# The Gated DeltaNet convolution inputs in 512-column products with sums in PSUM, and a new order of casts and low parts

## The reference

```python
proj = jnp.einsum('bsd,de->bse', hn, w_in[l])
(fq, fk, fv, ff, gq, gk, gv, ga, gb, gz, gate_fox, gate_gdn) = split_in(proj)
log_f = jax.nn.log_sigmoid(ff.astype(jnp.float32) + fox_f_bias[l].astype(jnp.float32))
qkv = jax.nn.silu(causal_dwconv(jnp.concatenate([gq, gk, gv], axis=-1), gdn_conv_w[l]))
cq, ck, cv = jnp.split(qkv, [GDN_K_WIDTH, 2 * GDN_K_WIDTH], axis=-1)
q = l2norm(cq.reshape(B, S, GDN_HEADS, GDN_HEAD_K))
k = l2norm(ck.reshape(B, S, GDN_HEADS, GDN_HEAD_K))
v = cv.reshape(B, S, GDN_HEADS, GDN_HEAD_V)
g = -jnp.exp(gdn_a_log[l].astype(jnp.float32)) * jax.nn.softplus(
    ga.astype(jnp.float32) + gdn_dt_bias[l].astype(jnp.float32))
beta = jax.nn.sigmoid(gb.astype(jnp.float32))
```

## Time and profile before

| | us |
|---|---|
| median of three runs (1611.69 to 1614.2) | 1613.13 |
| the profiled execution | 1614.05 |
| its span, first to last instruction | 1612.3 |
| TensorE busy in it | 1564.9 |
| VectorE busy | 629.7 |
| ScalarE busy | 499.2 |
| GpSimd busy | 291.2 |

### The profile page before, as it was taken

One profiled execution on the slowest core, in us unless ns is written; L12 is line 12 of the kernel. 1 busy time (PEld: TensorE's weight loads), 2 busy tenths in 40 slices (PEclk: granted clock), 3 DMA queues, 4 the chain that ended last, 5 costly groups with the idle time before them and its releaser, 6 DMA issues. The chain is left out here.

```text
span 1612.3 us, 21430 instructions
## 1 busy us (share of the span) xinstructions
PE 1564.9 (97%) x8406; PEld 882.2 (55%) x8406; DVE 629.7 (39%) x1177; ACT 499.2 (31%) x795; POOL 291.2 (18%) x179
## 2 busy tenths in 40 slices
PE   9999999999999999999999999999999999999998
PEld 8843333333333333323233233588899888888886
DVE  7742212121212212112121121396476456658752
ACT  6431111111111111111101111366556553467753
POOL 2600000000000000000000000274333323435552
PEclk9999999999999999999999999999999999999999
DMA  9699999999999999999999999644234234556552
GB/s 349 233 380 354 427 427 427 427 427 426 428 426 428 427 428 426 427 428 428 428 428 428 428 428 427 248 157 157 78 115 144 84 105 162 205 167 212 180 187 104
DMA packets 94889, 507.67 MB, mean 315 GB/s; under 512 B 10059, under 2 KB 35448, under 8 KB 70104
## 3 DMA queue, kind: packets, MB, share of 16 engines
q1 hardware_dynamic: 94568, 505.97, 77.8%
q10 hardware_dynamic: 240, 0.55, 0.1%
HBM read 505.46 MB, written 1.05 MB: 314 GB/s over the span
## 5 line engine op out<-in xcount | busy, mean ns | idle before, releaser
L190 POOL TENSOR_TENSOR low<-ring,high 128x1024 fp32r<-128x1024 f32 x81 | 201.7, 2491 | 1261.9 <-ACT high L187 1261.8
L1741 PE MATMUL ps<-ring,x 128*64 128x512 f32 x1536 | 341.9, 595 | 20.9 <-DMA ring<-in_w_up 20.9
L1741 PEld LDWEIGHTS ps<-ring,x 128*64 128x64 f32 x1536 | 106.0, 137 | 252.7 <-issue 207.0
L187 ACT CAST high<-ring 128x1024 fp32r<-128x1024 f32 x162 | 168.0, 1052 | 110.0 <-PE ps L1993 28.4
L1782 PE MATMUL ps<-ring,x 128*64 128x512 f32 x752 | 172.0, 600 | 1.2 <-issue 0.8
L190 DVE TENSOR_TENSOR low<-ring,high 128x1024 fp32r<-128x1024 f32 x81 | 107.4, 1326 | 95.0 <-ACT high L187 94.3
L1584 DVE TENSOR_SCALAR hT<-ps 128x512 f32<-128x512 f32 x32 | 22.1, 692 | 291.7 <-PE ps L1741 291.7
L1741 PE MATMUL ps<-extra,x 128*64 128x512 f32 x512 | 114.6, 595 | 5.8 <-DMA extra<-in_w_up 5.8
L1958 PE MATMUL ps<-hTb,high 128*128 128x512 f32 x464 | 116.4, 393 | 0.5 <-PEq L2917 0.5
L1782 PEld LDWEIGHTS ps<-ring,x 128*64 128x64 f32 x752 | 52.5, 138 | 100.7 <-issue 100.0
L1651 ACT COPY gpickT<-ps 128x256 f32<-128x256 f32 x32 | 11.9, 373 | 282.1 <-PE ps L1761 282.1
(11 more groups left out here) (518 smaller groups left out, 2302.8 us busy)
## 6 DMA issues: line engine op xcount, KB each, us to landing
ring<-in_w_down SPq DMA_DIRECT2D x52, 2048.0 KB, 32.7
ring<-in_w_gate SPq DMA_DIRECT2D x48, 2048.0 KB, 31.2
ring<-in_w_up SPq DMA_DIRECT2D x47, 2048.0 KB, 31.1
ring<-in_w_in SPq DMA_DIRECT2D x22, 2048.0 KB, 7.9
extra<-in_w_gate SPq DMA_DIRECT2D x16, 2048.0 KB, 31.4
extra<-in_w_up SPq DMA_DIRECT2D x16, 2048.0 KB, 29.7
extra<-in_w_down SPq DMA_DIRECT2D x14, 2048.0 KB, 34.5
ring<-in_w_up SPq DMA_DIRECT2D x24, 1024.0 KB, 7.2
```

What stands on the lines that cost most here:

```text
L187: eng.copy(hi, self.raw(u)).then_inc(self.sem("high_split"), 1)
L190: eng.tensor_tensor(lo, self.raw(u), hi.bitcast(F32), ALU.subtract).then_inc(self.sem(who + "_split"), 1)
L1741: last = pe.matmul(bank[h * CAP:(h + 1) * CAP, :], xg[:, c, kh, :], w[:, c, h * 512:(h + 1) * 512], start=False, stop=kh == 1 and c == 3)
```

## The change

The pieces gq, gk and gv of both groups go through `columns_wide`; each unit has a bank of its own, and the bank plan is stretched accordingly. fq, fk, fv and gz stay as they were. The convolution works chunk by chunk (256 columns, one unit): ScalarE copies the bank's second half to the new buffer `whole_conv`, VectorE adds it onto the first half in PSUM, ScalarE writes the last tap with a scaled copy, VectorE adds the three other taps. Two chunks overlap on VectorE. The semaphores `chunk_taken` and `chunk_sum` count the hand-overs, and the w_up stage goes on counting on them. On ScalarE, in group 0, the copy of the gate columns stands between q chunks 1 and 2; k chunks 0 and 1 stand in the gate rows, between the first exponentials and the logarithms; the casts `ahead(7)` and `ahead(9)` stand ahead of the logarithms and after the gate exponentials. On VectorE k chunks 0 and 1 stand ahead of the wait for the logarithms, a low part `ahead(9)` after `beg`, and the rows' low parts move from ahead of gv to between its chunks 1 and 2.

```diff
@@ -1846,7 +1846,9 @@
     for hg in range(2):
-        for w in ("gq", "gk", "gv", "fq", "fk"):
+        for w in ("gq", "gk", "gv"):
+            piece("columns", [(w, hg, q) for q in range(4)])
+        for w in ("fq", "fk"):
             piece("columns", (None, (w, hg, 0), None, (w, hg, 1)))
...
@@ -1864,6 +1866,7 @@
 UNITS_GROUP, UNITS_E, UNITS_OUT = 28, 56, 88
+CONV_CHUNKS = 24
 
...
@@ -2057,6 +2060,7 @@
     gz = sb("gz", [P, NT, 512])
+    whole = sb("whole_conv", [P, 2, S])
     XT = sb("XT", [P, NT, HG, P])
...
@@ -2111,11 +2115,11 @@
 
-    banks.plan(*[("nm", j) for j in range(4)], "rt", ("rw", 0), ("rw", 1))
+    banks.plan(*[("nm", j) for j in range(4)])
     for hg in range(2):
-        banks.plan(("gq", hg, 0), ("gq", hg, 1), *([("oT", 0, 0), ("oT", 0, 1)] if hg else []),
-                   ("gk", hg, 0), ("gk", hg, 1),
-                   ("gv", hg, 0), ("gv", hg, 1), *([] if hg else ["cols"]),
+        banks.plan(*[("gq", hg, q) for q in range(4)], *([("oT", 0, 0), ("oT", 0, 1)] if hg else ["rt"]),
+                   ("gk", hg, 0), *([] if hg else [("rw", 0), ("rw", 1)]), *[("gk", hg, q) for q in range(1, 4)],
+                   *[("gv", hg, q) for q in range(4)], *([] if hg else ["cols"]),
                    ("fq", hg, 0), ("fq", hg, 1), *[("ss", hg, j) for j in range(4)], *[("rb", hg, h) for h in range(HG)],
...
@@ -2183,7 +2187,9 @@
                     chain(act.activation(temp[:, b, :], temp[:, b, :], ACT.Exp, scale=-1.0))
-                ahead(6)
+                for q in range(2):
+                    chunk(0, 1, q)
+                ahead(7)
                 for b in (TC, TD):
...
@@ -2194,6 +2200,7 @@
                 act.activation(temp[:, KD, 0:P], temp[:, KD, 0:P], ACT.Exp).then_inc(sem("eg_rows"), 1)
+                ahead(9)
                 banks.moved(act, ("rw", 1))
...
@@ -2207,26 +2214,45 @@
 
+            def chunk(hg, w, q):
+
+                n = 12 * hg + 4 * w + q
+                bank = banks.take(act, (("gq", "gk", "gv")[w], hg, q))
+                if n >= 2:
+                    act.wait_ge(sem("chunk_sum"), n - 1)
+                act.copy(whole[:, q % 2, :], bank[:, S:2 * S]).then_inc(sem("chunk_taken"), 1)
+                ahead(UNITS_GROUP * hg + 4 * w + q + 1)
+                act.wait_ge(sem("chunk_sum"), n + 1)
+                at = 17 + 24 * 3 + 8 * w + HG * hg + q
+                act.activation(gT[:, w, q, :], bank[:, 0:S], ACT.Copy, scale=prm2[:, at:at + 1])\
+                    .then_inc(sem("chunk_taken"), 1)
+
+            def silu(hg, w, j):
+
+                for q in (2 * j, 2 * j + 1):
+                    banks.moved(act, (("gq", "gk", "gv")[w], hg, q))
+                part = gT[:, w, 2 * j:2 * j + 2, :]
+                act.activation(part, part, ACT.Silu).then_inc(sem("g_silu"), 1)
+
             for hg in range(2):
 
                 u0 = UNITS_GROUP * hg
                 for w in range(3):
                     if hg and w == 1:
                         delta_high(0)
-                    for j in range(2):
-                        if hg == w == 0:
-                            if j == 0:
-                                ahead(4)
-                                gate_columns()
-                            else:
-                                ahead(5)
-                        else:
-                            ahead(u0 + 4 * w + 2 * j + 3)
-                        banks.moved(act, (("gq", "gk", "gv")[w], hg, j))
-                        part = gT[:, w, 2 * j:2 * j + 2, :]
-                        act.activation(part, part, ACT.Silu).then_inc(sem("g_silu"), 1)
+                    for q in range(4):
+                        if hg or w != 1 or q >= 2:
+                            chunk(hg, w, q)
+                        if hg == w == 0 and q == 1:
+                            gate_columns()
+                        if q == 1 and w and not (hg == 0 and w == 1):
+                            silu(hg, w - 1, 1)
+                    silu(hg, w, 0)
                     if hg == w == 0:
+                        ahead(5)
+                        silu(hg, 0, 1)
                         gate_rows()
+                silu(hg, 2, 1)
 
...
@@ -2434,8 +2460,7 @@
                 banks.release(last, ("rw", 0))
-                units.ahead(v, "low0", 6)
-                conv(1, "gk", 0, (0,))
+                conv(1, "gk", 0, range(2))
                 v.wait_ge(sem("rows_ln"), 2)
...
@@ -2454,27 +2479,35 @@
                 v.tensor_tensor(temp[:, BEG, P:S], temp[:, BEG, P:S], rowp[:, BETA, P:S], ALU.mult).then_inc(sem("beg"), 1)
-
-            def conv(w, name, hg, halves=(0, 1)):
-
-                for j in halves:
-                    units.ahead(v, "low0", UNITS_GROUP * hg + 4 * w + 2 * j + 2)
-                    bank = banks.take(v, (name, hg, j))
-                    for i in range(4):
-                        for a in range(2):
-                            ch = 8 * w + HG * hg + 2 * j + a
-                            c = gT[:, w, 2 * j + a, :]
-                            tap = prm2[:, 17 + 24 * (3 - i) + ch:18 + 24 * (3 - i) + ch]
-                            if i == 0:
-                                last = v.tensor_scalar(c, bank[:, a * S:(a + 1) * S], tap, None, ALU.mult)
-                            else:
-                                last = v.scalar_tensor_tensor(c[:, i:], bank[:, a * S:(a + 1) * S - i], tap, c[:, i:],
-                                                              ALU.mult, ALU.add)
-                            if i < 3:
-                                chain.mark(last)
-                        if i < 3:
-                            chain.wait()
-                    banks.release(last, (name, hg, j))
+                units.ahead(v, "low0", 9)
+
+            def conv(w, name, hg, chunks=range(4)):
+
+                def tap(q, i):
+
+                    bank = banks.take(v, (name, hg, q))
+                    c = gT[:, w, q, :]
+                    at = 17 + 24 * (3 - i) + 8 * w + HG * hg + q
+                    return v.scalar_tensor_tensor(c[:, i:], bank[:, 0:S - i], prm2[:, at:at + 1], c[:, i:], ALU.mult, ALU.add)
+
+                for q in [*chunks, None]:
+                    before = chunks[-1] if q is None else q - 1
+                    n = 12 * hg + 4 * w + before + 1
+                    if before >= chunks[0]:
+                        v.wait_ge(sem("chunk_taken"), 2 * n)
+                        chain.mark(tap(before, 1))
+                    if q is not None:
+                        bank = banks.take(v, (name, hg, q))
+                        v.wait_ge(sem("chunk_taken"), 2 * n + 1)
+                        v.tensor_tensor(bank[:, 0:S], bank[:, 0:S], whole[:, q % 2, :], ALU.add).then_inc(sem("chunk_sum"), 1)
+                    if before >= chunks[0]:
+                        chain.wait()
+                        chain.mark(tap(before, 2))
+                    if q is not None:
+                        units.ahead(v, "low0", UNITS_GROUP * hg + 4 * w + q + 1)
+                    if before >= chunks[0]:
+                        chain.wait()
+                        banks.release(tap(before, 3), (name, hg, before))
 
...
@@ -2492,14 +2525,17 @@
                     gate_rows()
-                conv(1, "gk", hg, (0, 1) if hg else (1,))
+                conv(1, "gk", hg, range(4) if hg else range(2, 4))
                 if hg == 0:
+                    conv(2, "gv", hg, range(2))
                     v.wait_ge(sem("row_high"), 2)
                     v.tensor_tensor(row_low[:, GC:BETA + 1, :], rowp[:, :, :], row_high[:, GC:BETA + 1, :].bitcast(F32),
                                     ALU.subtract).then_inc(sem("row_low"), 1)
                     v.tensor_tensor(row_low[:, NEGC, :], temp[:, TB, :], row_high[:, NEGC, :].bitcast(F32),
                                     ALU.subtract).then_inc(sem("row_low"), 1)
-                conv(2, "gv", hg)
+                    conv(2, "gv", hg, range(2, 4))
+                else:
+                    conv(2, "gv", hg)
 
...
@@ -2638,6 +2674,9 @@
 
+            def wide(u, name, hg, before=None, first=None):
+                columns_wide(pe, units, banks, u, [(name, hg, q) for q in range(4)], hTb, before, first)
+
             def both_t(u, name, hg, before=None):
...
@@ -2726,13 +2765,13 @@
                 u0 = UNITS_GROUP * hg
-                both_f(u0 + 0, "gq", hg, None, None if hg else splits_ready(k, pe, banks, "nm"))
+                wide(u0, "gq", hg, None, None if hg else splits_ready(k, pe, banks, "nm"))
                 if hg:
                     outputs_transposed(0)
                 else:
                     gate_columns()
-                both_f(u0 + 4, "gk", hg, None if hg else gate_rows)
-                both_f(u0 + 8, "gv", hg)
+                wide(u0 + 4, "gk", hg, None if hg else gate_rows)
+                wide(u0 + 8, "gv", hg)
                 if hg == 0:
...
@@ -3079,15 +3118,15 @@
                 if u >= 2:
```

(14 more changed lines are left out.)

## The result

The changed kernel takes 1616.55 us (median; 1613.95 to 1617.71) against 1613.44 for the kernel before (1611.16 to 1614.91) on the same chip: ratio 1.0019, 95% interval 1.0013 to 1.0026, so about 3.1 us more. The forecast was 1614.6, with 1607 to 1618 as its range, and "within 0.2%" as the likeliest case; the narrower range of the sum itself, 1612 to 1616, missed by 0.55. In a second comparison the same kernel had 1.0026 (1.0015 to 1.0036).

A forecast was written before the change was run, and what follows sets the result against it. The prediction took TensorE, busy 97% of the span, as the bound, with a 4.6 us hole at unit 12. Group 0 losing 2.6 and group 1 gaining 1.1 gave +1.5 on 1613.13: 1614.6 us, range 1607 to 1618.

The forecast's parts named there:

- Wide products: Groups 0 and 1: a wide unit takes 2.79 us instead of 2.88, saving 1.1 us in group 1.
- estimate of 0.24: Group 1's saving in us if a pair of products saves only 2.5 ns; the forecast would be 0.8 us longer.
- The rival that wide products are no faster: Wide products take as long as narrow ones, 1.1 us missing: 1615.7 us, inside the forecast; no chance of its own.
- Steps 1 to 5: Group 0 to unit 10: VectorE idle 4.1 us before k chunk 0, TensorE waiting 3 to 4.3 us at unit 10.
- Step 6: Group 0 at unit 13: TensorE waits about 1.5 us, then 0.5 for GpSimd's low part.
- a low clock after unit 10 is mostly swallowed here: Group 0 at unit 13: later waits there absorb most of the time a low clock after unit 10 costs.
- Step 7: End of group 0: silu, two casts and first square put the square sums at 1098.4 against 1095.82; loss taken as 2.6.
- What follows: After group 0's square sums: the shift passes on unchanged, group 1 has no waits and gains 1.1 us.
- 4.1 us of cover ... and the shift goes on one for one: After group 0's square sums: scaled q and k are ready 4.1 us before use, hiding ScalarE's 1 us extra lateness.
- The sum: Whole kernel: 2.6 lost in group 0 less 1.1 gained in group 1, +1.5 us, median 1614.6 us.
- TensorE-bound: Rival in group 0: ScalarE comes in time and no unit waits, 6.6 us less, 1606.5 us; chance 0.13.
- the slower rival: The clock falls to 0.50 at group 0's square sums, costing 1.6 us: 4.2 more in all, 1617.3 us; chance 0.21.

The follow-up runs named there:

- third version of the new order: Against the second version: q's squares behind v chunk 2, k's behind v chunk 3, VectorE copies fq's two banks instead of ScalarE; 1609.62 us against 1611.77 before, ratio 0.9985.
- second version: Against the first version of the new order: rows' low parts, row selector, v's first silu, squares and unit 17's cast moved; ratio to before 0.9992.
- first version of the new order: Changed kernel with casts and VectorE's low parts two units further ahead from k chunk 2, gate rows before silus, other reordering; ratio to before 1.0004.

## Why the prediction was right, and where it was not

*Wide products* (0.09 a unit): right. Twelve units of group 1 gave 0.99, expected 1.1. The estimate of 0.24 from the Trainium skill's page "TensorE: Matmul & The Clock Gate", section "Wait — 56ns, not 53.3ns?", differs from the measurement, and the measurement decides. The rival that wide products are no faster falls with it.

*Steps 1 to 5*: right within 0.6 us. VectorE's idle time before k chunk 0 was 4.64 for 4.1, unit 10's low part was done 38.4 us after unit 0 where the walk had 37.6 to 38.9, and TensorE waited 3.76 where 3 to 4.3 was forecast.

*Step 6* named two waits at unit 13 (1.5 and 0.5); in the profile above neither came. Its cast was done 47.55 us after unit 0 (47.3 walked), but the low clock behind unit 10 held TensorE until 48.28 (45.8 walked). That was chance: in the second profile of the same kernel unit 11's eight wide products took 2.39 us, not 3.41, TensorE came sooner, and both waits came, 0.23 on the cast and 0.32 on GpSimd's low part. The square sums were at 58.8 in both, so "a low clock after unit 10 is mostly swallowed here" was right; the waits were sized too long.

*Step 7*: right. Square sums +2.75 for +2.6, the wait there 1.70. The experiment with the squares ahead of the casts gives the two casts 1.5 of it, and the early low part of unit 10 shows that this end, not unit 10, sets the time in this kernel.

*What follows* is the step that failed, and with it the sum is 1 us short. "4.1 us of cover ... and the shift goes on one for one" looked at the scaled q and k, which are used first. The next use has less: the k transposes claim the third bank that VectorE frees. Before, that was 1.8 us ahead of them (its multiplication ended at 1113.88, the transposes began at 1115.66). After, ScalarE and VectorE are 1 us later than TensorE, as the text says itself, and both blocked decay products of 2.15 and 2.11 us now stand ahead of that bank, where only one did before:

```profile
1110.85 2.16 DVE L2533 TENSOR_TENSOR egb<-egb,gT 128x128 f32<-128x128 f32 x1
...
1113.47 0.41 DVE L2530 TENSOR_TENSOR xn<-xn,ps 128x256 f32<-128x256 f32 x1
...
1115.66 2.18 PE L2774 MATMUL ps<-ident,gT 128*128 128x128 f32 x16
```

These rows are of before (VectorE's first decay product, its third bank, TensorE's transposes); after has its rows above. So TensorE waits 0.71 there, and by the table the shift grows by 0.96 at the k transposes, of which 0.86 are left at unit 28. The experiment with the decay products behind takes out 0.66.

*The sum*: 2.6 - 1.1 = +1.5 was forecast; the distances give 2.75 + 0.86 - 0.99 = +2.6. Behind group 1 lies 0.24 more, from a wait of 0.23 at 1362.05 on a cast, behind a load that landed 0.2 later; before it is under 0.2, in the third version of the new order 0.52. Together 2.9, and the interval of the measured 3.1 (2.1 to 4.2) takes that in. Why the ratio lies above what the distances say for every kernel here, by 0.2 to 2.6 us, 1.1 in the mean, is not located: one profile of each can't show it. One thing to ask is the granted clock: the runs of before in the second comparison took 1613.3 to 1614.6 us at a mean granted clock of 0.995 and 1611.1 to 1612.3 at 0.998.

*The rivals*: TensorE-bound did not come by itself, but the third version, with the order changed and fq's copy on VectorE, gives 3.8 of the 6.6 us that it counted; its argument ("VectorE's work doesn't grow") was sound (busy 624.6 us after, 629.7 before), and "ScalarE's order" was the right reason against it. The clock at the square sums stayed at 1.00, so the slower rival's mechanism fell; that its time of 1617.3 was nearer than the forecast is luck. Its "no row shows a wait of that length" overlooked the kernel before at 141 to 143 us (last section).

## What to carry to other kernels

When a stage is handed from one engine to a chain of two, the chain's end can set the time, and a long wait of the main engine in the middle can be worth nothing: before removing it, ask what that engine meets next. When a shift is passed on, check the cover of every later claim, the banks too, not only that of the first use. In group 1, without gate rows, the wide products paid at once; in group 0 only when casts, table loads and silus of ScalarE stood where VectorE wasn't waiting for its copy, and VectorE had taken over two copies.

## What the runs showed of the hardware

The granted clock against the length of one wait: it stayed at 1.00 through waits of 1.23 and 0.79 (third version), 1.54 (gate rows ahead) and 1.70 (after, at the square sums); it was 0.50 after 1.88 (cast of unit 11 later), 2.78, 3.70 and more. Two waits of 1.47 and 1.10, with 1.2 us of products between them (first version of the new order), were followed by 0.50 too. But the length of a wait doesn't settle it. In the expert loop of the changed kernel the clock stayed at 1.00 through a wait of 1.90 for a load:

```profile
1013.69 3.65 PE L1741 MATMUL ps<-ring,x 128*64 128x512 f32 x16 [1.90 <-DMA ring<-in_w_up]
...
1012.00:1016.00 4.00, 2.31 (x12) 1.00 0.94 399
```

And the same two waits of 1.57 and 0.83 us, behind the same code, were followed by 0.50 in the kernel before (141.10 and 142.58, first row) and not in the changed one (140.64 and 142.13, second row):

```profile
144.00:146.00 2.00, 2.00 (x7) 0.51 1.09 467
...
144.00:146.00 2.00, 2.00 (x12) 1.00 0.97 418
```

So a low clock behind a wait under 2 us comes in one execution and not in another, and one profile doesn't show whether a kernel has it.

GpSimd's row selector, built beside VectorE's row chain in the first new order, made that chain 5.8 us long, from its first operation to the end of line 2494, instead of 3.4: the first addition took 1.17 us, and 0.41 in the second version, without it.

```profile
1067.53 1.17 DVE L2483 SCALAR_TENSOR_TENSOR xn<-xn 8x256 f32<-8x256 f32 x1
```

```profile
1067.73 0.41 DVE L2483 SCALAR_TENSOR_TENSOR xn<-xn 8x256 f32<-8x256 f32 x1
```

VectorE's operations that read PSUM and one SBUF tile kept their 0.41 to 0.43 us beside GpSimd's low parts (line 2566 above), while line 2569, with both operands in SBUF, took 2.15 for 0.28 and line 2475, with one, 2.18 for 0.27.
